# Splitting w_out and v on GpSimd in attention's first tiles, and loading the first q rows one stage earlier

## What is computed

```python
h = layer_norm(x)
proj = h @ w_in                       # q (8 heads of 64), k and v (2 heads), x_lru, y_lru
q, k = rope(rms_norm(q)), rope(rms_norm(k))
attn = softmax(q @ k.T / 8) @ v       # each sequence attends to itself
lru  = (rg_lru_forward(conv(x_lru)) + rg_lru_backward(conv(x_lru))) * gelu(y_lru)
merged = concat(rms_norm(attn) * attn_out_g, rms_norm(lru) * lru_out_g)
h = layer_norm(alpha * h + merged @ w_out)
out = layer_norm(alpha * h + hier_moe(h))      # 16 experts, 2 a row
```

## Time and profile before

| | us |
|---|---|
| median of 3 runs | 1604.24 (1603.88 to 1604.75) |
| the profiled execution, its time | 1599.9 |
| its span, first to last instruction | 1598.1 |
| TensorE busy in it | 1444.6 (90%) |
| VectorE busy | 1126.0 (70%) |
| ScalarE busy | 928.1 (58%) |
| GpSimd busy | 481.1 (30%) |

### The profile page before, as it was taken

How to read it: one execution, slowest core, us unless ns; L and a number is a source line. 1 busy time by engine, 2 the same in 40 slices (tenths; PEclk the granted TensorE clock), 3 DMA queues, 4 the chain that set the end, 5 groups by cost and what they waited for, 6 DMA issues and landing times. The chain is left out here.

```text
span 1598.1 us, 30295 instructions
## 1 busy us (share of the span) xinstructions
PE 1444.6 (90%) x8945; PEld 1258.7 (79%) x8947; DVE 1126.0 (70%) x2198; ACT 928.1 (58%) x1624; POOL 481.1 (30%) x347
## 2 busy tenths in 40 slices
PE   6999989999996999999999999975899999999940
PEld 5999977777765899999999999963777788777820
DVE  8787547999977888888888888877444334444237
ACT  4444338788776666666666666633565445555325
POOL 1212124565440011111121111131454433555318
PEclk9999999999998999999999999996999999999965
DMA  8865641544454112111112121127798787786576
GB/s 290 297 229 195 231 144 70 192 165 151 166 174 163 52 61 79 60 59 59 61 67 92 65 73 60 47 96 239 230 277 251 205 246 189 216 266 151 110 228 256
DMA packets 126214, 250.09 MB, mean 156 GB/s; under 512 B 24498, under 2 KB 77746, under 8 KB 126132
## 3 DMA queue, kind: packets, MB, share of 16 engines
q1 hardware_dynamic: 94000, 160.97, 29.2%
q0 software_dynamic: 12528, 45.99, 12.3%
q10 hardware_dynamic: 19604, 42.09, 7.0%
HBM read 154.35 MB, written 94.67 MB: 156 GB/s over the span
## 5 line engine op out<-in xcount | busy, mean ns | idle before, releaser
L1755 DVE TENSOR_TENSOR d_probs_t_lo<-d_pt_ps,d_probs_t_hi 128x512 fp32r<-128x512 f32 x256 | 165.0, 686 | 63.6 <-ACT d_probs_t_hi L1669 62.0
L1669 ACT ACTIVATE d_probs_t_hi<-d_pt_ps 128x512 fp32r<-128x512 f32 x256 | 139.2, 596 | 95.6 <-PE d_pt_ps L1550 89.3
L1731 DVE TENSOR_REDUCE d_neg_max<-d_s_ps 128x1 f32<-128x1024 f32 x128 | 155.5, 1215 | 3.4 <-PE d_s_ps L1539 3.4
L122 PE MATMUL acc<-k_hi,wl_hi 128*128 128x256 f32 x512 | 145.8, 285 | 4.4 <-DVE k_lo L597 4.4
L1652 ACT ACTIVATE d_probs<-d_s_ps,d_neg_max 128x1024 f32<-128x1024 f32 x128 | 143.4, 1121 | 4.3 <-DVE d_neg_max L1731 4.3
L122 PE MATMUL e_a_ps<-up_hi,e_xt_hi 128*128 x336 | 137.1, 408 | 9.7 <-DVE e_xt_lo L2591 5.0
L123 PE MATMUL acc<-k_lo,wl_hi 128*128 128x256 f32 x512 | 144.9, 283 | 0.0
L124 PE MATMUL acc<-k_hi,wl_lo 128*128 128x256 f32 x512 | 144.9, 283 | 0.0
L1550 PE MATMUL d_pt_ps<-ident,d_probs 128*128 128x128 f32 x1024 | 132.9, 273 | 4.7 <-ACT d_probs L1652 3.2
L1564 PE MATMUL d_ot_ps<-d_probs_t_hi,d_v_split 128*128 128x256 f32 x512 | 127.4, 287 | 8.3 <-DVE d_probs_t_lo L1755 8.3
L123 PE MATMUL e_a_ps<-up_lo,e_xt_hi 128*128 x336 | 133.4, 397 | 0.0
(11 more groups left out here) (414 smaller groups left out, 4089.3 us busy)
## 6 DMA issues: line engine op xcount, KB each, us to landing
up_raw<-in_exp_w SPq DMA_DIRECT2D x32, 1024.0 KB, 9.5
down_raw<-in_exp_w SPq DMA_DIRECT2D x16, 1024.0 KB, 14.1
d_h_tile<-h_dram SPq DMA_DIRECT2D x16, 522.0 KB, 4.8
h_dram<-v_all ACTq DMA_DIRECT2D x16, 512.0 KB, 3.2
ht_hi_dram<-k_hi ACTq DMA_DIRECT2D x8, 1024.0 KB, 4.3
ht_lo_dram<-k_lo ACTq DMA_DIRECT2D x8, 1024.0 KB, 6.7
d_q_tile<-q_dram SPq DMA_DIRECT2D x16, 512.0 KB, 4.3
h_dram<-l_h_tile SPq DMA_DIRECT2D x16, 512.0 KB
```

Source lines behind the costliest of these rows:

```text
L122: pe.matmul(out, lhs[0], rhs[0], start=first, stop=False)
L1669: act.activation(pt_hi[:, c * HALF:(c + 1) * HALF, h % 2], pt_ps[c][:], ACT.Copy).then_inc(pth_done[c], 1)
L1731: dve.tensor_reduce(nm[:, u, h:h + 1], s_ps[h % 2][:], AX, ALU.max, negate=True).then_inc(nm_done, 1)
L1755: dve.tensor_tensor(pt_lo[:, part, h % 2], pt_ps[c][:], pt_hi[:, part, h % 2].bitcast(F32), ALU.subtract)\
```

## The change

- The q rows of tiles 0 and 1 are loaded in `qkv_lru`: SP waits for the last scan, then issues both loads, then goes on to the store of the last recurrent unit. The two tiles of q are laid in `spare`'s place for that, and the order of the buffers of `attend` is such that nothing else there takes it. Their semaphores `q_` belong to the scope `kept`, which ends behind `attend`: clearing them brings a second meeting of all engines there.
- ScalarE first runs an exponential of one column, then v's high part, then head 0's exponentials.
- GpSimd makes v's low part, then all eight blocks of w_out, those of the recurrent half (4 to 7) first. A block is three instructions, each waiting for the one before: gained rows as fp32r into `w_hi`, gained rows in place, the difference into `w_lo`. There are four raw buffers instead of two.
- ScalarE and VectorE no longer split w_out in tile 0. The reciprocal norms of the recurrent branch are cut in two: `lru_norms_start` (a sum and four small scalar operations) stands in head 3 behind the router's gained columns, the nine steps of `rsqrt_steps` stand in head 6. The router's low part and rows move to head 4.
- TensorE's first wait for `ones_made` moves to the router sums. Before the first product with w_out it waits for four blocks, in head 3 of tile 1 for all eight.

```diff
...
...
+            ahead = kept.enter_context(semaphores(nc, "q_"))
+            q_in = [ahead(f"q_loaded{u}") for u in range(2)]
...
+                with ExitStack() as places:
+                    q_t = [places.enter_context(nc.sbuf_tensor(f"q_tile{u}", [P, NQ, P], F32R)) for u in range(2)]
...
+                        w_out, r_w, w_r, h_dram, (hr, k_st, qk_g, qk_small, hi_room), q_t, q_in)
...
+                if g == NU:
+                    sp.wait_ge(scans_done, NU)
+                    sp.wait_ge(q_stored, 16 * (TILES.index(1) + 1))
+                    for u in range(2):
+                        sp.dma_start(q_ahead[u][:].rearrange("p h t -> p (h t)").bitcast(F32), q_dram[u]).then_inc(q_in[u], 16)
                 store(g - 1)
...
+        vs = sb("v_split", [P, NT, NKV, 2, HD], F32R)
+        pr = [sb(f"probs{j}", [P, SEQ]) for j in range(2)]
...
+        sb("place_of_q_tiles", [P, 2 * NQ * P])
         w_hi = sb("wo_hi", [P, KD, DW], F32R)
...
-        raw = [s_t[1][:, 0:D], h1[:]]
+        ON_POOL = [4, 5, 6, 7, 0, 1, 2, 3]
+        raw = [s_t[1][:, 0:D], h1[:], sb("wo_raw_pool0", [P, D])[:], sb("wo_raw_pool1", [P, D])[:]]
...
+            def load_for_pool(i):
+                rows = slice(ON_POOL[i] * P, (ON_POOL[i] + 1) * P)
+                sp.dma_start(raw[i % 4], w_out[0, rows, :]).then_inc(raw_in[i % 4], 16)
...
             sp.sem_inc(h1_stored, 32)
-            load_q(0, 0)
-            load_q(1, 1)
...
-                for k in range(2):
-                    sp.dma_start(raw[k], w_out[0, k * P:(k + 1) * P, :]).then_inc(raw_in[k], 16)
+                for i in range(len(raw)):
+                    load_for_pool(i)
                 load_y(0)
...
-            for k in range(2, KD):
-                sp.wait_ge(lo_made, k - 1)
-                sp.dma_start(raw[k % 2], w_out[0, k * P:(k + 1) * P, :]).then_inc(raw_in[k % 2], 16)
+            for i in range(4, KD):
+                sp.wait_ge(pool_lo_made, i - 3)
+                load_for_pool(i)
...
         def _(pe):
-            pe.wait_ge(ones_made, 2)
-
...
             def sum_router():
+                pe.wait_ge(ones_made, 2)
                 for k in range(KD):
...
                 if h == 0:
                     if not late:
                         pe.wait_ge(rows_read, 2)
-                        pe.wait_ge(lo_made, KD)
                         pe.wait_ge(rl_made, 1)
+                        pe.wait_ge(pool_lo_made, 4)
                     pe.wait_ge(yl_done, t)
...
+                if h == 3 and not late:
+                    pe.wait_ge(pool_lo_made, KD)
                 if h in (3, 5, 6):
                     project(0, (3, 5, 6).index(h))
...
             act.sem_inc(xn_done, 1)
-            act.activation(vs[:, :, :, 0], v_all[:].rearrange("p t (g d) -> p t g d", g=NKV), ACT.Copy).then_inc(vh_made, 1)
+            act.activation(warm[:], ident[:, 0:1], ACT.Exp)
...
-                if not post:
-
-                    act.wait_ge(raw_in[h % 2], 16 * (h // 2 + 1))
-                    act.wait_ge(out_g_in, 32)
-                    act.activation(w_hi[:, h, 0:D], raw[h % 2], ACT.Copy, scale=out_g[:, h:h + 1]).then_inc(hi_made, 1)
-                    if h == 1:
-                        act.wait_ge(wg_made, 1)
-                        act.activation(w_hi[:, :, D:], w_rg[:], ACT.Copy).then_inc(rh_made, 1)
+                if not post and h == 4:
+                    act.wait_ge(wg_made, 1)
+                    act.activation(w_hi[:, :, D:], w_rg[:], ACT.Copy).then_inc(rh_made, 1)
                 beside()
...
-            run_heads(act, lambda: exp(0, 0, 0), head, aux)
+            def first():
+                act.activation(vs[:, :, :, 0], v_all[:].rearrange("p t (g d) -> p t g d", g=NKV), ACT.Copy).then_inc(vh_made, 1)
+                exp(0, 0, 0)
+
+            run_heads(act, first, head, aux)
...
-            def lru_norms():
-                link = Chain(dve, dve_link)
-                link(dve.tensor_reduce(lru_tmp[:].rearrange("p (s c) -> p s c", s=SEQS),
-                                       lru_sums[:].rearrange("p (s f) c -> p s c f", s=SEQS), AX, ALU.add))
-                link(dve.tensor_scalar(lru_var[:], lru_tmp[:], ALPHA ** 2 / LW, LN_EPS * ALPHA ** 2, ALU.mult, ALU.add))
-                rsqrt(dve, link, lru_var[:], rl[:], lru_tmp[:], wide=True)
+            lru_link = Chain(dve, dve_link)
+
+            def lru_norms_start():
+                lru_link(dve.tensor_reduce(lru_tmp[:].rearrange("p (s c) -> p s c", s=SEQS),
+                                           lru_sums[:].rearrange("p (s f) c -> p s c f", s=SEQS), AX, ALU.add))
+                lru_link(dve.tensor_scalar(lru_var[:], lru_tmp[:], ALPHA ** 2 / LW, LN_EPS * ALPHA ** 2, ALU.mult, ALU.add))
+                rsqrt_guess(dve, lru_link, lru_var[:], rl[:], lru_tmp[:])
             def first():
-                lru_norms()
                 neg_max(0, 0, 0)
                 neg_max(0, 0, 1)
-                dve.wait_ge(vh_made, 1)
-                dve.wait_ge(out_g_in, 32)
-                dve.tensor_tensor(w_rg[:], w_r[:], out_g[:].unsqueeze(2).broadcast_to([P, KD, RW]), ALU.mult).then_inc(wg_made, 1)
-                dve.tensor_tensor(vs[:, :, :, 1], v_all[:].rearrange("p t (g d) -> p t g d", g=NKV),
-                                  vs[:, :, :, 0].bitcast(F32), ALU.subtract).then_inc(vl_made, 1)
...
                 if nxt[1]:
                     neg_max(*nxt[1])
                 if not post:
-                    dve.wait_ge(hi_made, h + 1)
-                    dve.scalar_tensor_tensor(w_lo[:, h, 0:D], raw[h % 2], out_g[:, h:h + 1], w_hi[:, h, 0:D].bitcast(F32),
-                                             ALU.mult, ALU.subtract).then_inc(lo_made, 1)
-                    if h == 1:
+                    if h == 3:
+                        dve.wait_ge(out_g_in, 32)
+                        dve.tensor_tensor(w_rg[:], w_r[:], out_g[:].unsqueeze(2).broadcast_to([P, KD, RW]), ALU.mult).then_inc(wg_made, 1)
+                        lru_norms_start()
+                    if h == 4:
                         dve.wait_ge(rh_made, 1)
                         dve.tensor_tensor(w_lo[:, :, D:], w_rg[:], w_hi[:, :, D:].bitcast(F32), ALU.subtract).then_inc(rl_made, 1)
-                    if h == 2:
+                    if h == 6:
+                        rsqrt_steps(dve, lru_link, lru_var[:], rl[:], lru_tmp[:], wide=True)
+                    if h == 4:
                         dve.wait_ge(rows_done, 1)
                         dve.wait_ge(rows_in, 64)
                         dve.tensor_copy(r_rows[:, 0], m_ps[:, 0:RW]).then_inc(rows_read, 1)
...
+            def split_w(i):
+                k, part = ON_POOL[i], raw[i % 4]
+                pool.wait_ge(raw_in[i % 4], 16 * (i // 4 + 1))
+                pool.tensor_scalar(w_hi[:, k, 0:D], part, out_g[:, k:k + 1], None, ALU.mult).then_inc(pool_gained, 1)
+                pool.wait_ge(pool_gained, 2 * i + 1)
+                pool.tensor_scalar(part, part, out_g[:, k:k + 1], None, ALU.mult).then_inc(pool_gained, 1)
+                pool.wait_ge(pool_gained, 2 * i + 2)
+                pool.tensor_tensor(w_lo[:, k, 0:D], part, w_hi[:, k, 0:D].bitcast(F32), ALU.subtract).then_inc(pool_lo_made, 1)
+
+            pool.wait_ge(vh_made, 1)
+            pool.tensor_tensor(vs[:, :, :, 1], v_all[:].rearrange("p t (g d) -> p t g d", g=NKV),
+                               vs[:, :, :, 0].bitcast(F32), ALU.subtract).then_inc(vl_made, 1)
+            pool.wait_ge(out_g_in, 32)
+            for i in range(len(ON_POOL)):
+                split_w(i)
             pool.sem_inc(hg_done, 2)
...
```

More of the change, by code:

```diff
@@ L192, in build @@
                         v_all, q_dram, lru_wa, lru_wx, xc_dram, y_dram, lru_dram, lru_rows[3], quarter_decay, nhalf_decay, lru_sums,
-                        w_out, r_w, w_r, h_dram, (hr, k_st, qk_g, qk_small, hi_room))
+                        w_out, r_w, w_r, h_dram, (hr, k_st, qk_g, qk_small, hi_room), q_t, q_in)
             sem = to_routing.enter_context(semaphores(nc, "d_"))
@@ L1331, in need, with attend @@
         eng.wait_ge(sem, value)
-def attend(nc, sem, w_out, attn_g, lru_g, ln_g, ln_b, router_bg, router_be, r_w, w_r, ident,
+def attend(nc, sem, q_t, q_in, w_out, attn_g, lru_g, ln_g, ln_b, router_bg, router_be, r_w, w_r, ident,
            k_hi, k_lo, v_all, lru_dram, lru_sums, h_dram, q_dram, h1_dram, sum_dram, logits,
@@ L1364, in attend @@
         ones = sb("ones", [P, P])
-        vs = sb("v_split", [P, NT, NKV, 2, HD], F32R)
-        q_t = [sb(f"q_tile{u}", [P, NQ, P], F32R) for u in range(2)]
-        pr = [sb(f"probs{j}", [P, SEQ]) for j in range(2)]
-        pt_hi = sb("probs_t_hi", [P, TPS, 2, P], F32R)
-        pt_lo = sb("probs_t_lo", [P, TPS, 2, P], F32R)
         ot = sb("o_t", [P, 2 * P])
@@ L1402, in attend @@
         out_g_in = sem("out_g_loaded")
-        raw_in = [sem(f"wo_raw_loaded{j}") for j in range(2)]
+        raw_in = [sem(f"wo_raw_loaded{j}") for j in range(len(raw))]
```

(5 more changed lines are left out.)

17 lines of the change are left out of this document (10 added, 7 removed).

## The result

| | before | after |
|---|---|---|
| median, us | 1604.49 | 1625.45 |
| lowest to highest | 1603.88 to 1608.25 | 1619.72 to 1626.36 |
| the profiled execution, its time | 1599.9 | 1625.29 |
| its span | 1598.1 | 1623.5 |

The ratio is 1.0127, with a 95% interval of 1.0106 to 1.0148. The change makes the kernel slower, as forecast, but by 21 us instead of 11.6, and 1625.45 lies just above the range of 1597.5 to 1624. It also lost the time in another place than the walk of the prediction said.

What follows compares the result with a forecast made beforehand. Tile 0 was taken as bound by the wait for q and three-engine chains, tile 1 by TensorE. Held operations 8.9 + clock 2.0 + second meeting 0.7 = +11.6 us on 1604.24 gave 1615.8 us, range 1597.5 to 1624.

Steps and rivals of the forecast that it cites:

- the walk of the prediction: Tile 0, heads 3 to 7: small VectorE operations held by GpSimd move tile 1 from 528.5 to 537.4, +8.9 us.
- What bounds tile 0: Tile 0 of attention: not TensorE, but 5.5 us of idle until q lands and each head pair's three-engine chain.
- the start: Start of attention: q loads issued near 469 cost nothing, so TensorE starts at 485.45, 4.0 us gained.
- v's low part: GpSimd at attention's start: 4.5 to 4.7 us, 488.85 to 493.4, wanted at 496.7, so covered.
- GpSimd's list: Eight w_out blocks of 4.8 us from 493.4, multiplication estimated at 1.1 us: in time for TensorE in tile 1.
- some 12 more: Tile 1: added us if a multiplication takes 2.36 us, as small operations there then meet GpSimd too.
- What GpSimd does to VectorE: Tile 0: each small VectorE operation waits for GpSimd's whole instruction, a chain paying one per link; called decisive.
- its arm without holding: Tile 0 with no VectorE operation held by GpSimd: tile 1 begins at 522.1 instead of 528.5, -6.4 us.
- GpSimd becomes TensorE's bound: Head 3 of tile 1: 2.36 us multiplications, list until 552, 18 us stall, +12.3, 1616.5 us; chance 0.05.
- Nothing is held: Tile 0: small VectorE operations slip past GpSimd, -6.4 + 0.7 = -5.7, 1598.5 us; chance 0.17.
- The clock: Around tile 1's start: half clock after TensorE's idle gap before head 7's product, counted 2.0 us.
- The second meeting: Behind attention: clearing the `q_` semaphores adds a meeting of all engines, 0.7 us, hidden by nothing.

Runs made afterwards that it cites:

- e2_tt: Changed kernel with GpSimd's two multiplications per w_out block as two-input operations, the gain's column repeated: 1613.98 us, ratio 1.0058 to the kernel before.
- e9_both: Changed kernel without each block's second GpSimd multiplication, and with all reciprocal norms ahead of the first maximum: 1599.78 us, ratio 0.9984 to the kernel before.
- e8_one_mult: Changed kernel without the second GpSimd multiplication of each w_out block, that gain left out of the low part: 1608.46 us, ratio 1.0039 to the kernel before.
- e1_const: Changed kernel with GpSimd's two multiplications per w_out block taking constant 2.7 instead of the per-row gain: 1621.02 us, ratio 1.0093 to the kernel before.
- e4_four: Changed kernel with w_out blocks 4 to 7 back on ScalarE and VectorE, norms' start ahead of first maximum, steps in head 1: 1594.52 us, ratio 0.9967 to before.
- e3_q_only: Kernel before plus only the early q load, its buffers and semaphores, and the one-column exponential ahead: 1599.56 us, ratio 0.9979 to the kernel before.
- e10_v_low: As e3_q_only, with v's low part on GpSimd, w_out's blocks staying on ScalarE and VectorE: 1599.48 us, ratio 0.9974 to the kernel before.

## Why the prediction was wrong, and where it was right

- **What bounds tile 0, the start, v's low part: right.** Scores at 485.83 (forecast 485.4 plus a stage that opens 0.45 later), v's low part 4.55 us and covered.
- **GpSimd's list: wrong, and this is the step that failed.** The sum was 8.9 (held operations) + 2.0 (clock) + 0.7 (meeting), with TensorE's wait for the list at nothing; the wait took 19.67 us and its half clock 2.3. The multiplication was taken at 1.1 us between 0.9 and 2.36. It takes 2.85, outside both ends. The error was to treat as a bracket: a memset reads nothing, and that a one-input instruction can't take longer than a two-input one was never shown by a row. "Block 7 near 533, in time" was 559.6, too late. The range hangs on the same step: for 2.36 us, its own upper bound, the prediction gives "some 12 more" than 1615.8, but the range ends at 1624.
- **What GpSimd does to VectorE: half right.** The earlier trace rows show VectorE held by two-input GpSimd instructions, and there it is mostly so in every run (2.22, 1.82, 1.75 us, ending 0.02 to 0.03 behind; what starts between two of them slips through). Not all: the norms' sum over columns takes 0.25 us at 507.32 in e2_tt and a scalar operation on one column 0.14 at 529.20 in e9_both, each beside a two-input GpSimd instruction. I carried it over to one-input ones. These let it through from about 1.1 us on: seen at 519.59 in after, in e8_one_mult (1.14), and in e1_const (1.06). Now and then one is held late: a scalar operation at 506.86 in after, 1.92 us into an in-place multiplication, waits for its end, two just before it don't; one 1.82 us into a multiplication of e8_one_mult waits too. The row in after, and GpSimd's beside it:

```profile
504.94 2.85 POOL L1948 TENSOR_SCALAR l_h_tile<-l_h_tile,d_out_g 128x1024 f32<-128x1024 f32 x1
506.86 0.96 DVE L102 TENSOR_SCALAR d_lru_rstd<-d_lru_tmp 128x16 int32<-128x16 int32 x1
```

What decides that stays open. The Trainium skill ("SBUF — State Buffer", section "SBUF: two separate sides") says that the first to start has the shared path for the whole instruction; these runs mostly agree for two-input GpSimd instructions and not for one-input ones, and the measurement decides. The walk's +8.9 us was -3.4; its arm without holding, 522.1 (36.7 behind 485.4), is reached by e9_both (35.8 behind the start). That the forecast said "slower" and that 1625.45 is only 1.45 us beyond the range is luck: its largest term had the wrong sign, and one of 22 us that it left out took its place.
- **The rival "GpSimd becomes TensorE's bound" was the cause**, named with its place (head 3 of tile 1) and a wait of 18 us, and got 0.05. Measured: 19.67. Its 1616.5 is low since tile 1 came at 525.1 and not 522, the list ended at 559.6 and not 552, and the half clock behind the wait wasn't priced (2.3). It "decides from a multiplication of about 1.2 us on" (where nothing is held), 0.1 above my value; with bounds of 0.9 to 2.36 that alone asked for far more than 0.05.
- **"Nothing is held"** fell on the same price. With both losses away, attention ends 5.2 us earlier than before in e9_both and 6.1 in e4_four; with the 0.4 of the meeting that is near this rival's -5.7. So the gain exists, though a part of it, 2.1 us in e3_q_only, needs only the early load.
- **The clock: right in kind.** Ahead of tile 1 it was at half from about 523.5 to 526.9 (0.88 in the window from 522, 0.50 from 524, 0.77 from 526), behind a gap of 2.65 us that ended at 522.42. The larger loss was behind the wait.
- **The second meeting:** 0.7 forecast, 0.4 measured. In e3_q_only and e10_v_low the routing starts 2.41 and 2.50 behind attention, 0.8 to 0.9 more than before; why more there, I didn't look into.

## What to carry to other kernels

When work moves to an engine on which no row shows that very instruction form, the price is unknown on both sides: ask first from what price on its list becomes somebody's bound, and give that case the chance that the ignorance deserves. A list that ends well ahead of its reader (four blocks instead of eight) cost no wait, though it isn't shown that those four gained anything over none. Small chained VectorE operations don't belong beside a busy GpSimd; and removing one of two stacked limits shows the other, so change both before judging either.

## What the runs showed of the hardware

- GpSimd, 128x1024 in float32: one input times a value per row 2.85 us, times a constant 2.77, two full inputs mostly 2.34 to 2.41, two inputs of which one is a repeated value 1.89.
- A small VectorE operation with both inputs in SBUF, or a scalar one, is mostly held by a two-input GpSimd instruction to its end (2.22 us instead of 0.17), by a one-input one mostly to about 1.1 us behind its start; the exceptions are named above. It goes the other way too: in e4_four GpSimd's multiplications take up to 4.34 us beside VectorE's 128x1024 low parts.
- VectorE's low parts of the probabilities, with one input in PSUM, take 1.29 us a pair beside GpSimd in tile 0, as against 1.28 without it.
